# Encoder trunk on one core: S5 states with real and imaginary parts in columns, attention probabilities scaled ahead of their turning

## The reference

```python
# B) grouped-query attention: 8 query heads of 64, 2 key/value heads, 128 queries at a time
s = jnp.einsum('bkgqd,bksd->bkgqs', q_blk, kh) * scale
p = jax.nn.softmax(s, axis=-1)
return jnp.einsum('bkgqs,bksd->bkgqd', p, vh)

# C) S5: 16 groups x 16 channels, 64 complex states a group, forward and backward
bu = jnp.einsum('bsgc,gpc->sbgp', ug, b_bar)
_, states = lax.associative_scan(_linear_combine, (a, bu), axis=0, reverse=(d == 1))
y = y + jnp.real(jnp.einsum('sbgp,gcp->bsgc', states, c_mat)).reshape(B, S, S5_WIDTH)
# then z = gelu(y); z * sigmoid(z @ w_glu + b_glu)
```

## Time and profile before

| | |
|---|---|
| median of 3 runs | 1585.46 us (1584.69 to 1585.79) |
| profiled execution: its own time | 1585.26 us |
| its span, first to last instruction | 1583.4 us |
| PE busy, PEld, DVE, ACT, POOL | 1530.6, 785.9, 621.3, 425.2, 377.4 us |
| chain that ended last: PE, DMA, DVE, ACT | 82%, 9%, 6%, 2% |
| mean granted TensorE clock | 0.997 of 2.4 GHz |

### The profile page before, as it was taken

How to read it: one execution, slowest core, us unless ns; L and a number is a source line. 1 busy time by engine, 2 the same in 40 slices (tenths; PEclk the granted TensorE clock), 3 DMA queues, 4 the chain that set the end, 5 groups by cost and what they waited for, 6 DMA issues and landing times.

```text
span 1583.4 us, 20219 instructions
## 1 busy us (share of the span) xinstructions
PE 1530.6 (97%) x8156; PEld 785.9 (50%) x8156; DVE 621.3 (39%) x1244; ACT 425.2 (27%) x762; POOL 377.4 (24%) x432
## 2 busy tenths in 40 slices
PE   8999999999999999998999999999999999999986
PEld 4655566555444444443347546655554444444432
DVE  2697546462122212311427965474522122123114
ACT  3654641211111111111235547403111111111102
POOL 4671790000000000000265637600000000000003
PEclk9999999999999999999999999999999999999999
DMA  9300403959999999999950003059699999999997
GB/s 394 145 0 14 147 1 89 426 220 424 427 426 428 426 428 426 428 425 429 363 247 1 1 29 132 1 175 409 240 426 427 425 427 426 428 427 428 427 426 305
DMA packets 58546, 470.02 MB, mean 297 GB/s; under 512 B 19481, under 2 KB 19609, under 8 KB 30258
## 3 DMA queue, kind: packets, MB, share of 16 engines
q1 hardware_dynamic: 51202, 452.37, 68.9%
q0 software_dynamic: 7104, 16.24, 2.7%
q10 hardware_dynamic: 144, 0.07, 0.0%
HBM read 447.69 MB, written 26.74 MB: 300 GB/s over the span
## 4 chain that ended last, share of the span: by engine, by line
PE 82%; DMA 9%; DVE 6%; ACT 2%; issue 1%; POOL 0%; SPq 0%; POOLq 0%; DVEq 0%; ACTq 0%
PE bank L1029 24%; PE bank L1068 12%; PE bank L670 10%; PE bank L1019 9%; PE bank L801 7%; DMA ring<-wu 5%; DMA ring<-wd 2%; PE bank L745 2%; PE bank L732 2%; PE bank L662 2%; PE bank L762 2%; PE bank L1006 1%; PE bank L1053 1%; PE bank L656 1%; PE bank L878 1%
## 5 line engine op out<-in xcount | busy, mean ns | idle before, releaser
L2266 POOL DMA_INDIRECT expert_rows<-raw_qd,store_rows x60 | 58.8, 980 | 1002.5 <-ACT raw_qd L1470 944.3
L1029 PE MATMUL bank<-ring,hbuf 128*64 128x512 f32 x640 | 281.2, 593 | 6.8 <-DMA ring<-wu 6.8
L1030 PE MATMUL bank<-ring,hbuf 128*64 128x512 f32 x640 | 281.4, 593 | 0.0
L2018 DVE COPY raw_qd<-bank 128x256 f32<-128x256 f32 x64 | 27.2, 424 | 642.0 <-PE bank L1053 642.0
L670 PE MATMUL bank<-hbuf,ring 128*128 128x512 f32 x480 | 210.1, 595 | 0.6 <-DVE hbuf L1533 0.6
L1029 PEld LDWEIGHTS bank<-ring,hbuf 128*64 128x64 f32 x640 | 86.8, 137 | 185.4 <-issue 185.1
L1029 PE MATMUL bank<-raw_qd,hbuf 128*64 128x512 f32 x372 | 163.7, 592 | 3.6 <-DMA hbuf<-wu 3.6
L1068 PE MATMUL bank<-ring,raw_qd 128*64 128x512 f32 x352 | 160.4, 598 | 5.7 <-DVE raw_qd L2018 3.1
L1070 PE MATMUL bank<-ring,raw_qd 128*64 128x512 f32 x352 | 160.5, 598 | 0.0
L1019 PE MATMUL bank<-raw_qd,x 128*128 128x192 f32 x896 | 159.5, 332 | 0.0
L1463 ACT ACTIVATE raw_qd<-bank 64x512 f32<-64x512 f32 x64 | 37.8, 590 | 416.7 <-PE bank L1030 416.7
(11 more groups left out here) (401 smaller groups left out, 2247.2 us busy)
## 6 DMA issues: line engine op xcount, KB each, us to landing
ring<-wg SPq DMA_DIRECT2D x38, 2048.0 KB, 19.2
ring<-wd SPq DMA_DIRECT2D x38, 2048.0 KB, 19.8
ring<-wu SPq DMA_DIRECT2D x34, 2048.0 KB, 22.2
ninth_slot<-wd SPq DMA_DIRECT2D x20, 2048.0 KB, 20.2
raw_qd<-wg SPq DMA_DIRECT2D x18, 2048.0 KB, 19.7
hbuf<-wu SPq DMA_DIRECT2D x18, 2048.0 KB, 23.3
ring<-w_in SPq DMA_DIRECT2D x6, 2048.0 KB, 19.4
raw_qd<-wg SPq DMA_DIRECT2D x6, 1792.0 KB, 12.5
```

The costliest lines, as they stand in the source:

```text
L1029: mm(pb[2 + par][0:CAP, :], tokens[:, k, :], gates[k], start=(k == 0), stop=(k == KT - 1))
L1030: last = mm(pb[2 + par][CAP:P, :], tokens[:, k, :], ups[k], start=(k == 0), stop=(k == KT - 1))
L2266: G.indirect_dma_start(out=half_rows, out_offset=bass.IndirectOffsetOnAxis(ap=store_i[:, e:e + 1], axis=0), in_=y_sb[e % 2], in_offset=Non ...
```

## The change

In attention, DVE multiplies the probabilities with the inverse sums before they are turned: `TS(p, p, p_inv[...])`, one instruction for each of the two heads, in place in `p_sb`. `turned(u)` waits for that (`pn`). The two products L756, the copy L1705 and `n_sb` are gone, and `unit_out` is a copy.

In S5, a bank holds the real parts of four columns of chunks and then the imaginary parts, and the two halves of the partitions hold different groups. The exchange is now a reversed index in the free dimension, so `half_swap`, `sine_parts` and the eight products against it go. The inputs are 64 wide on both sides, 16 products a quarter in place of 8. The tables hold 16 columns of angles in place of 32. `early(3)` to `early(7)` move forward; `final(0)` and `final(1)` are made tile by tile as `o_c` comes.

```diff
@@ shapes
-        cosT = hbuf[:, 0:2048].rearrange("p (d k) -> p d k", d=DG)
-        sinT = hbuf[:, 2048:4096].rearrange("p (d k) -> p d k", d=DG)
+        cosT, sinT = (hbuf[:, at:at + G5 * NK].rearrange("p (j k) -> p j k", j=G5) for at in (0, 1024))
+        in_halves = lambda ap: [ap[:, 512 * i:512 * i + 512].rearrange("p (r j k) -> p r j k", r=2, j=4) for i in range(4)]
+        turned_by_sine = in_halves(hbuf[:, 2048:4096])
-        X_BANK = [(pb[4], pb[5]), (pb[0], pb[1]), (pb[2], pb[3]), (pb[4], pb[5])]
+        X_BANK = (pb[4], pb[0], pb[2], pb[3])
...
@@ tensor_program
             def turned(u):
-                pe.wait_ge(s["ex"], on("ex") + u + 1)
+                pe.wait_ge(s["pn"], on("pn") + u + 1)
             def values(u):
-                pe.wait_ge(s["pn"], on("pn") + u + 1)
-                for i in range(2):
-                    mm(bank[HD * i:HD * i + HD, P:2 * P], p_inv[u % 2][:, i:i + 1].broadcast_to([P, HD]), ident,
-                       start=True, stop=True)
-                for i in range(8):
-                    dg = 8 * q + i
-                    u = U5[:, dg % G5, :] if dg < G5 else U5[:, dg % G5, ::-1]
-                    last = mm(X_BANK[q][0][:, NK * i:NK * i + NK], Bt[:, dg, :], u, start=True, stop=True)
+                for part in range(2):
+                    for i in range(4):
+                        for half in range(2):
+                            g = 4 * (q % 2) + i + G5 // 2 * half
+                            u = U5[:, g, :] if q < 2 else U5[:, g, ::-1]
+                            at = NK * (4 * part + i)
+                            last = mm(X_BANK[q][HD * half:HD * half + HD, at:at + NK],
+                                      Bt[:, G5 * (q // 2) + g, HD * part:HD * part + HD], u, start=True, stop=True)
...
+            for q in range(4):
+                chunk_inputs(q)
+            for n in range(2, 6):
+                early(n)
             last.then_inc(s["yt"], 1)
-            early(5)
             early(6)
+            early(7)
...
-            early(7)
-            pe.wait_ge(s["o_c"], on("o_c") + 2)
+            def first_finals():
+                for k in range(6, KT):
+                    pe.wait_ge(s["o_c"], on("o_c") + k - 5)
+                    for n in range(2):
+                        if n == 1 and k == 6:
+                            pe.wait_ge(s["gx"], on("gx") + 4)
+                        last = mm(pb[n][:, :], mixed[k][:, 0:P], w_o[n][:, k, :], start=(k == 6), stop=(k == KT - 1))
...
@@ DVE program
-                V.tensor_copy(n_sb[u % 2], bank[:, P:2 * P]).then_inc(s["pn_e"], 1)
-                dve.wait_ge(s["pn_e"], on("pn_e") + u + 1)
-                TT(aq[pair][:, P * b:P * b + P], bank[:, 0:P], n_sb[u % 2], ALU.mult).then_inc(s["o_b"], 1)
+                V.tensor_copy(aq[pair][:, P * b:P * b + P], A_BANK[u % 2][:, 0:P]).then_inc(s["o_b"], 1)
                 dve.wait_ge(s["ex"], on("ex") + u + 1)
-                V.reciprocal(p_inv[u % 2], p_sum[u % 2]).then_inc(s["pn"], 1)
+                link(V.reciprocal(p_inv[u % 2], p_sum[u % 2]))
+                for i in range(2):
+                    p = p_sb[u % 2][:, i, :]
+                    ins = TS(p, p, p_inv[u % 2][:, i:i + 1], None, ALU.mult)
+                ins.then_inc(s["pn"], 1)
             def rotated(q):
+                a = X_BANK[q][:, :].rearrange("p (r j k) -> p r j k", r=2, j=4)
+                TT(T2[q], a[:, ::-1], both_parts(sinT, q), ALU.mult)
+                TT(T1[q], a, both_parts(cosT, q), ALU.mult).then_inc(s["xr"], 1)
             def scanned(q):
+                TT(T1[q][:, RE], T1[q][:, RE], T2[q][:, RE], ALU.add)
+                link(TT(T1[q][:, IM], T1[q][:, IM], T2[q][:, IM], ALU.subtract))
...
+                TT(turned_by_sine[q], T2[q][:, ::-1], both_parts(sinT, q), ALU.mult)
+                link(TT(T1[q], T2[q], both_parts(cosT, q), ALU.mult))
+            def states(q):
+                for half in range(2):
+                    h = slice(HD * half, HD * half + HD)
+                    g = G5 * (q // 2) + 4 * (q % 2) + G5 // 2 * half
+                    for part, op in ((RE, ALU.subtract), (IM, ALU.add)):
+                        rows = S5[HD * part:HD * part + HD, g:g + 4, :]
+                        ins = TT(rows[:, :, 1:NK] if q < 2 else rows[:, :, NK - 2::-1], T1[q][h, part, :, 0:NK - 1],
+                                 turned_by_sine[q][h, part, :, 0:NK - 1], op)
...
...
@@ POOL program
-            c1, s1, c2, s2 = Wi[:, 0, :], Wi[:, 1, :], Wi[:, 2, :], Wi[:, 3, :]
+            c1, s1, c2, s2 = (Wi[:, i, 0:G5] for i in range(4))
+            by_pairs(c1, pv_cos)
+            by_pairs(s1, pv_sin)
...
```

More of the change, by code:

```diff
@@ L282, in trunk @@
             qk="PE: attention scores", mx="DVE: row maxima",
-            ex="ACT: probabilities", pn="DVE: inverse sums of a unit", pt="PE: probabilities transposed",
-            pt_e="ACT: transposed probabilities evacuated", pv="PE: attention output of a unit, inverse sums by row",
-            pn_e="DVE: inverse sums by row evacuated", o_b="DVE: o_b of a unit", u5="u stored, loaded by chunk, then S5 chunk matrix loaded",
+            ex="ACT: probabilities", pn="DVE: probabilities of a unit times their inverse sums", pt="PE: probabilities transposed",
+            pt_e="ACT: transposed probabilities evacuated", pv="PE: attention output of a unit",
+            o_b="DVE: o_b of a unit", u5="u stored, loaded by chunk, then S5 chunk matrix loaded",
             ang="Pool: S5 angles, denominators",
@@ L290, in trunk @@
             bt_v="DVE: even banks of Bt evacuated",
-            xin="PE: S5 chunk inputs of a quarter", xr="DVE: sine, cosine parts of a quarter", xw="PE: sine parts with halves swapped",
+            xin="PE: S5 chunk inputs of a quarter", xr="DVE: sine and cosine parts of a quarter",
             z="DVE: S5 quarters scanned",
-            zs="PE: S5 states swapped", xs="DVE: S5 states", y5="PE: S5 outputs", y5_e="ACT: S5 outputs, first half",
+            xs="DVE: S5 states", y5="PE: S5 outputs", y5_e="ACT: S5 outputs, first half",
             y5_v="DVE: S5 outputs, second half", yt="PE: S5 outputs feature-major", ge="DVE: gelu argument", gx="ACT: gelu, then GLU tanh", z5="DVE: gelu",
@@ L1771, in vector_program @@
             early(2)
+            states(1)
             rotated(3)
             scanned(2)
+            states(2)
             early(3)
             scanned(3)
-            V.memset(S5[:, 0:G5, 0], 0.0)
-            V.memset(S5[:, G5:DG, NK - 1], 0.0)
-            for q in range(4):
-                r = slice(8 * q, 8 * q + 8)
-                dve.wait_ge(s["zs"], on("zs") + q + 1)
-                link(TT(T2[:, r, :], pb[q][:, :].rearrange("p (d k) -> p d k", d=8), sinT[:, r, :], ALU.mult))
-                to = S5[:, r, 1:NK] if q < 2 else S5[:, r, NK - 2::-1]
-                ins = TT(to, T1[:, r, 0:NK - 1], T2[:, r, 0:NK - 1], ALU.subtract)
-            ins.then_inc(s["xs"], 1)
+            states(3).then_inc(s["xs"], 1)
             early(4)
@@ L1789, in vector_program @@
                           pb[5][:, :].rearrange("p (g t c) -> p g t c", g=4, t=SC)).then_inc(s["y5_v"], 1)
+            early(5)
             dve.wait_ge(s["yt"], on("yt") + 1)
@@ L2258, in pool_program @@
             pool.wait_ge(s["ho"], on("ho") + 2)
-            link(G.tensor_copy(rho, pv_rho8[:, :, None].broadcast_to([P, DG, NK])))
+            rho_pairs = Wi[:, 0, 0:G5]
+            pool.wait_ge(s["bc"], on("bc") + 3)
+            by_pairs(rho_pairs, pv_rho8)
+            rho_parts = rho.rearrange("p (q r j) k -> p q r j k", q=4, r=2)
+            for part in range(2):
+                ins = G.tensor_copy(rho_parts[:, :, part], rho_pairs.rearrange("p (q j) -> p q j", q=4)[:, :, :, None]
+                                    .broadcast_to([P, 4, 4, NK]))
+            link(ins)
             G.memset(rho[:, :, 0], 0.0).then_inc(s["bc"], 1)
@@ L2355, in constants @@
     put("head_ones", (p // HD) == (q // HD))
-    put("half_swap", p == (q + HD) % P)
     put("before", p < q)
@@ L2380, in constants @@
     put("is_im", p >= HD)
-    put("sign", np.where(p < HD, 1.0, -1.0))
     put("eps", EPS)
```

83 lines of the change are left out of this document (31 added, 52 removed).

## The result

The changed kernel takes 1642.92 us (median of 4, 1639.81 to 1644.07); the kernel before took 1585.62 us beside it. The ratio is 1.0352, with a 95% interval from 1.0337 to 1.0367: 3.5% slower. The forecast was 1639 us.

The account below looks back on a forecast made before the run. PE bounds the kernel (busy 97%, chain on it 82%). Attention +61.4, clock +3, S5 -9.4 and tables -1.2 give +53.8 on a 1583.4 us span, 1637.2, so 1639 us; 8-in-10 range 1600 to 1665.

Parts of the forecast that it names:

- The likeliest case: Attention: each scaling beside POOL waits for one POOL product, some 8.7 us a unit, 1639 us in all; chance 0.74.
- A product in attention saved on PE: Attention: the removed spreading of inverse sums saves PE 0.33 us a unit, for a period of 3.0 us.
- Which unit the last product serves: Attention, layer 0: POOL's twelfth product serves unit 9's first scaling; unit 9 is turned at about 235.6, 32.6 us later.
- POOL held back by 0.2 a turn, 2.4 us: Attention: each scaling delays POOL some 0.2 us, 2.4 over its twelve products, so POOL ends at 234.6 in layer 0.
- Low clock, 1.5 a layer: Attention: PE's clock falls while it waits, costing 1.5 us a layer behind the wait, +3 in all.
- S5, -4.7 a layer: S5 stage: early(5) ahead of the outputs saves 5.15 us, less 0.5 of new waits; -9.4 in both layers.
- Tables, -0.6 a layer: HGRN gates: shorter POOL doublings block DVE for less time, 0.6 us a layer, -1.2 in all.
- Experts as a block: Experts: they move with the end of the mixer, so mixer gains or losses arrive whole, with 0 added.
- Rival 1: Attention: a unit's two scalings go through in one turn, one POOL product plus 0.5 us a unit, 1604 us; chance 0.11.
- Rival 2: Attention: no contention, scalings stay near 0.5 us beside POOL, 10.3 us gained a layer in all, 1565 us; chance 0.09.
- Rival 3: Attention: the low clock stays, units 9 to 15 take 5.9 us, 20 more a layer, 1678 us; chance 0.06.

Follow-up runs that it names:

- four_scalings: The changed kernel with each scaling of 128 x 512 cut into two of 128 x 256, four a unit: 1664.37 us, ratio 1.0493.
- pool_halved: The changed kernel with each of POOL's twelve products for Bt and Ct cut into two of half the length: 1607.86 us, ratio 1.0149.
- s5_alone: The changed kernel with attention as before the change, S5 and the tables as changed: 1575.75 us, ratio 0.9933 against the kernel before.

## Why the prediction was right

The likeliest case happened, and the steps that carried it held: each scaling beside POOL waits for one product, two in a row for one each, twelve turns (in layer 1 one of them for a head-norm product, which the prediction did not have), POOL all but undisturbed, PE waiting at `turned` and its clock low, and S5 a few us shorter. The runs show the cause: the same scalings in a form that isn't held cost nothing like it (64.8 us less).

The sum was 4 us low on the span, and part of that closeness is luck: terms that were off by 1 to 3 us pulled opposite ways. By its terms:

- *A product in attention saved on PE (0.33 a unit from the missing L756).* Wrong: the period behind POOL is 3.32 us, not 3.0, also in the kernel that is never held. The values wait for ACT's copy of the turned probabilities, 1.02 us, and L756 had lain beside that copy. The 0.37 us of the earlier trace rows was a wait with work in it, which I took for work. +1.5 in each layer.
- *Which unit the last product serves.* I had unit 3's first scaling ahead of POOL, so that unit 9 would follow 1.0 us behind POOL's end. With the shorter tables POOL started at 181.31, 0.26 us ahead of the scaling of 181.57, both scalings of unit 3 were held and POOL's last product served unit 8. Unit 9 then came a full unit behind POOL's end: +2.7 without the clock. POOL's earlier start gave back 1.1.
- *POOL held back by 0.2 a turn, 2.4 us.* It was 0.57 in all (50.39 - 49.82): -1.8.
- *Low clock, 1.5 a layer.* In layer 0 the unit behind the hold took 5.81 in place of 3.33, 2.5; in layer 1 it lay beside POOL.
- These make 31.9 + 1.5 + 2.7 - 1.1 - 1.8 + 1.0 = 34.2 in layer 0, where 34.6 were measured. In layer 1 unit 9 was turned 4.4 us behind POOL's end (1047.55, 1043.11) and not 1.5: unit 8 was turned first, at 1044.22, and a unit takes PE 3.3 us, which the 1.5 left out. +2.9, and +1.5 for L756; the turns cost POOL 2.1 less and the clock 1.5 less than forecast. That makes 31.3 + 0.8 = 32.1, and 31.6 were measured.
- *S5, -4.7 a layer.* -5.6 and -3.9. The chunk inputs take 1.0 us a quarter, 4.1 in all, 0.032 us an instruction, not 7.0 (the lower bound was 3.5); but PE's wait for the residual of `early(3)` grew to 2.94 from the 2 that I had, since VectorE sets that point, and behind it stood the clock in layer 1. The GLU side came as forecast (0.18 of waiting against 0.3).
- *Tables, -0.6 a layer.* The first turning of layer 0 came 0.5 us earlier (168.33, 168.85 before); from the features of layer 0 to the first turning of layer 1 it was 0.9 us less (650.85, 651.74), experts included.
- *Experts as a block.* +1.2 of 57.9 arose behind the features of layer 1.

Rival 1 (the pair in one turn) would have needed one product a unit with two scalings; the timeline of the changed kernel, four_scalings and pool_halved exclude it. Rival 2 did not occur with this form. In the kernel with accumulated output its condition holds, and there its 1565 is 13 us too low (1578): the PE saving is missing, some 5 us a layer, and in layer 1 the held head-norm product delays the scaling, 5.6 us. Rival 3 did not occur: the clock was back one unit behind the hold.

## What to carry to other kernels

Ahead of giving VectorE a pass over SBUF, list what GpSimd runs in that stretch and count turns: each held instruction waits out the rest of a GpSimd instruction, however small it is (here down to 128x16 and 128x256), and everything behind it on VectorE waits too. If the pass must be there, take a form that isn't held (operand in PSUM, or accumulated output), or few instructions against short GpSimd ones; but follow each wait that such an edit moves. And split a change of two parts: here a gain of 0.7% lay under a loss of 4.2%, and filling a wait of 3 us a layer on PE was worth nearly as much again (8.8 us beside 10.4).

## What the runs showed of the hardware

- The exclusion is not symmetric. VectorE's scaling of 0.44 us waited for up to a whole product of 3.8 to 4.4 us, and cost POOL 0.05 us; a tensor_tensor of 1.22 us cost it 0.8. With the scalings cut in four (0.29 us each) POOL's products took 3.81 and 4.26 us, as if alone.
- In layer 0 neither side got two turns running while both were waiting: 12 turns in the kernels with one, two and four VectorE instructions a unit, 24 in the one with POOL's products halved.
- A tensor_scalar of 128x512 with accumulated output or from PSUM (0.75 us in place of 0.44) ran beside POOL's products without any hold; a tensor_tensor of 128x1024 with two SBUF operands (1.22 us by itself) was held.
- In s5_alone, behind a wait of 2.95 us, PE's clock was full in layer 0 (5.42 us for an early group) and 0.65 on average in layer 1 (8.35 us).
